# Queries and keys of the two-mixer layers: transposed by VectorE blocks and on-chip transfers in place of TensorE

## What is computed

```python
proj = h @ w_in                       # 256 x 3088
aq, ak, av, gq, gk, gv, gr, g_low = jnp.split(proj, cuts, axis=-1)
aq = rope_partial(aq.reshape(B, S, 8, 64), pos)     # rotates 16 of the 64 numbers of a head
ak = rope_partial(ak.reshape(B, S, 8, 64), pos)
s  = einsum('bqhd,bqnhd->bhqn', aq, keys) * 64 ** -0.5   # masked, dilated; softmax; times values
a_out = rmsnorm(dilated_attention(aq, ak, av).reshape(B, S, 512), attn_out_norm)
o     = gla_chunked(gq, gk, gv, log_sigmoid(g_low @ w_gate_up + b) / 16)
g_out = rmsnorm(o, gla_out_norm) * silu(gr)
return concatenate([a_out, g_out]) @ w_out
```

## Time and profile before

| what | value |
|---|---|
| time, median of 3 runs | 1162.05 us (1161.86 to 1162.26) |
| the profiled execution, its own time | 1161.88 us |
| span of that execution, first to last instruction | 1160.1 us |
| TensorE busy | 1147.4 us, 99% of the span |
| VectorE busy | 779.3 us, 67% |
| ScalarE busy | 604.6 us, 52% |
| mean granted TensorE clock | 0.999 |

### The profile page before, as it was taken

One profiled execution on the slowest core, in us unless ns is written; L12 is line 12 of the kernel. 1 busy time (PEld: TensorE's weight loads), 2 busy tenths in 40 slices (PEclk: granted clock), 3 DMA queues, 4 the chain that ended last, 5 costly groups with the idle time before them and its releaser, 6 DMA issues.

```text
span 1160.1 us, 18219 instructions
## 1 busy us (share of the span) xinstructions
PE 1147.4 (99%) x6746; PEld 938.9 (81%) x6746; DVE 779.3 (67%) x1149; ACT 604.6 (52%) x896; POOL 46.5 (4%) x82
## 2 busy tenths in 40 slices
PE   8999999999999999999999999999999999999998
PEld 6887888888868888888778888888887778888886
DVE  5798666548897865554778777566466877865641
ACT  5555544425964554443556665445356666654530
POOL 0200000000001000000100100000010011000000
PEclk9999999999999999999999999999999999999999
DMA  9756876745734687664575169777548514877650
GB/s 328 252 169 195 277 217 217 218 147 180 254 93 145 203 271 218 217 208 158 166 238 155 33 195 296 218 214 224 163 147 272 164 56 145 275 222 219 211 171 36
DMA packets 186440, 225.82 MB, mean 195 GB/s; under 512 B 15954, under 2 KB 130298, under 8 KB 186369
## 3 DMA queue, kind: packets, MB, share of 16 engines
q1 hardware_dynamic: 181184, 213.07, 58.2%
q10 hardware_dynamic: 4896, 11.58, 3.1%
q0 software_dynamic: 288, 0.23, 0.1%
HBM read 212.22 MB, written 1.06 MB: 184 GB/s over the span
## 4 chain that ended last, share of the span: by engine, by line
PE 49%; DVE 2%; issue 0%; ACT 0%; POOL 0%; POOLq 0%; DVEq 0%; ACTq 0%
PE ps L601 15%; PE ps L603 14%; PE ps L602 14%; DVE w_lo L1602 1%; PE ps L973 1%; PE ps L769 1%; PE ps L1056 1%; PE ps L1031 1%; PE ps L777 0%; PE ps L1003 0%; PE ps L784 0%; PE ps L1023 0%; PE ps L1020 0%; DVE nbuf L1922 0%; PE ps L1002 0%
## 5 line engine op out<-in xcount | busy, mean ns | idle before, releaser
L1602 DVE TENSOR_TENSOR w_lo<-raw,w_hi 128x1024 fp32r<-128x1024 f32 x377 | 445.4, 1216 | 122.2 <-ACT w_hi L1201 119.1
L1201 ACT ACTIVATE w_hi<-raw 128x1024 fp32r<-128x1024 f32 x377 | 383.3, 1056 | 153.0 <-DMA raw<-w_down 35.2
L601 PE MATMUL ps<-w_hi,a_hi 128*128 128x512 f32 x1039 | 409.1, 394 | 2.2 <-DVE w_lo L1602 1.1
L603 PE MATMUL ps<-w_hi,a_lo 128*128 128x512 f32 x1039 | 404.8, 390 | 0.0
L602 PE MATMUL ps<-w_lo,a_hi 128*128 128x512 f32 x1039 | 404.5, 389 | 0.0
L601 PEld LDWEIGHTS ps<-w_hi,a_hi 128*128 128x128 f32 x1039 | 195.0, 188 | 44.7 <-DVE w_lo L1602 2.1
L603 PEld LDWEIGHTS ps<-w_hi,a_lo 128*128 128x128 f32 x1039 | 195.0, 188 | 41.2
L602 PEld LDWEIGHTS ps<-w_lo,a_hi 128*128 128x128 f32 x1039 | 195.2, 188 | 39.1
L601 PE MATMUL ps<-w_hi,h_hi 128*128 128x512 f32 x480 | 188.3, 392 | 0.5 <-DVE h_lo L2092 0.4
L603 PE MATMUL ps<-w_hi,h_lo 128*128 128x512 f32 x480 | 186.9, 389 | 0.0
L602 PE MATMUL ps<-w_lo,h_hi 128*128 128x512 f32 x480 | 186.9, 389 | 0.0
(11 more groups left out here) (224 smaller groups left out, 675.7 us busy)
## 6 DMA issues: line engine op xcount, KB each, us to landing
raw<-ffn_w_in SPq DMA_DIRECT2D x176, 256.0 KB, 4.1
raw<-w_in SPq DMA_DIRECT2D x96, 256.0 KB, 3.7
raw<-ffn_w_out SPq DMA_DIRECT2D x88, 256.0 KB, 3.1
raw<-w_gate SPq DMA_DIRECT2D x88, 256.0 KB, 3.3
raw<-w_up SPq DMA_DIRECT2D x88, 256.0 KB, 4.0
raw<-w_down SPq DMA_DIRECT2D x88, 256.0 KB, 3.2
moved<-turned SPq DMA_DIRECT2D x176, 64.0 KB, 2.6
raw<-od_w_in SPq DMA_DIRECT2D x40, 256.0 KB, 3.8
```

What stands on the lines that cost most here:

```text
L601: nc.tensor.matmul(ps[:, bank, :], hi, wh, start=first, stop=False)
L603: return nc.tensor.matmul(ps[:, bank, :], lo, wh, start=False, stop=last)
L1201: nc.scalar.activation(w_hi[:, v.slot, :], raw[:, v.slot, :], ACT.Copy).then_inc(w_high, 1)
L1602: V.tensor_tensor(w_lo[:, v.slot, :], raw[:, v.slot, :], w_hi[:, v.slot, :].bitcast(F32), ALU.subtract).then_inc(w_low, 1)
```

## The change

Only the two `hyb` layers change; the attention of layer 1 keeps its path (its semaphores are declared for that layer alone now).

- TensorE: the two `turn_qk` of a layer go, with their waits. `pair_logits` reads queries and keys from a new tile, `qk_moved`, after one wait for eight transfers.
- ScalarE: `q_part` goes; the factor -1/8 is put into the copy of chunk 1 from PSUM (`scale` of L1280), ahead of the rotation, which is linear.
- VectorE: `k_part` goes. New is `qk_squares`, at the end of `hyb_step` for c = 2, ahead of its last `feed`: four `transpose` instructions (32x32 blocks within 128x512) from `p_qk` to `qk_turned`. They write each output row of 32 numbers with a step of 64 bytes from one number to the next, since `qk_turned` keeps query or key, pair and token tile as the innermost indices.
- SP: new is `move_qk`, after the seventh unit of `w_out` (i == 6): a wait for `qk_squares`, then eight transfers from `qk_turned` to `qk_moved`, each 64 rows of 2 KB, so 128 KB each and 1 MB in all per layer.
- In `qk_moved` the tokens of one head and one tile are 16 numbers (64 bytes) apart. Both operands of the logits products are read with that step.

```diff
+        qk_moved, _ = place("qk_moved", [P, P, 2, 4, NT], F32)
+        qk_turned, _ = place("qk_turned", [P, 2, 2, 32, 2, 4, NT], F32, at_turned)
...
+            def move_qk(l):
+
+                sp.wait_ge(qk_done.sem, qk_done.at(l, 0))
+                for a in range(4):
+                    for par in range(2):
+                        sp.dma_start(qk_moved[64 * par:64 * (par + 1), 32 * a:32 * (a + 1), :, :, :].rearrange("p j s b t -> p (j s b t)"),
+                                     qk_turned[32 * a:32 * (a + 1), par, :, :, :, :, :].rearrange("p u j s b t -> p u (j s b t)")
+                                     ).then_inc(qk_in, 16)
...
                     load(Unit(U_B[l] + i), wo[k, :, 0:CH], wo[k, :, CH:D], False)
+                    if LAYERS[l] == "hyb" and i == 6:
+                        move_qk(l)
...
-                    if (c, q) == (4, 0):
-
-                        pe.wait_ge(z_out.sem, z_out.at(l, 0))
-                        pe.wait_ge(roped.sem, roped.at(l, 0))
-                        turn_qk(l, 0)
-                    if (c, q) == (5, 0):
-                        pe.wait_ge(q_out.sem, q_out.at(l, 1))
-                        turn_qk(l, 1)
...
+            def queries(l, i, j, t):
+                r = slice(HD * i, HD * (i + 1))
+                if LAYERS[l] == "hyb":
+                    return qk_moved[r, :, 0, j, t]
+                return qT[r, j, P * t:P * (t + 1)]
+
+            def keys(l, i, j, n):
+                r = slice(HD * i, HD * (i + 1))
+                if LAYERS[l] == "hyb":
+                    return qk_moved[r, :, 1, j, 0:n].rearrange("p n t -> p t n")
+                return kT[r, j, 0:P * n]
...
-                pe.wait_ge(q_out.sem, q_out.at(l, 1))
-                pe.wait_ge(k_out.sem, k_out.at(l, 1))
+                pe.wait_ge(qk_in, 128 * (hyb.index(l) + 1))
...
-                nc.scalar.activation(dst, bank, f).then_inc(a_out, 1)
+                scale = -SCALE if (LAYERS[l], c) == ("hyb", 1) else 1.0
+                nc.scalar.activation(dst, bank, f, scale=scale).then_inc(a_out, 1)
...
-                    if n == 5:
-                        q_part(l)
...
+            def qk_squares(l):
+
+                dve.wait_ge(roped.sem, roped.at(l, 0))
+                for part in range(2):
+                    for t in range(NT):
+                        dst = qk_turned[:, :, :, :, part, :, t].rearrange("p r u j b -> p b (r u) j")
+                        ins = V.transpose(dst, p_qk[:, t, CH * part:CH * (part + 1)])
+                        if (part, t) == (1, 1):
+                            ins.then_inc(qk_done.sem, 1)
...
+                if c == 2:
+                    qk_squares(l)
                 if c == 4:
-                    k_part(l)
                     feed(end)
```

More of the change, by code:

```diff
@@ L207, in blocks_kernel @@
         glu, _ = place("glu", [P, 2, NT, FC], F32)
-        turned, _ = place("turned", [P, LOOP, 4, 2, NT, 32], F32)
+        turned, at_turned = place("turned", [P, LOOP, 4, 2, NT, 32], F32)
         moved, _ = place("moved", [P, LOOP, 4, 2 * NT, 32], F32)
+        qk_moved, _ = place("qk_moved", [P, P, 2, 4, NT], F32)
+        qk_turned, _ = place("qk_turned", [P, 2, 2, 32, 2, 4, NT], F32, at_turned)
         assert top[0] <= nc.SBUF_PARTITION_SIZE_BYTES, top[0]
@@ L399, in blocks_kernel @@
         roped = stage("roped", 1, hyb)
-        qk_turned, q_out, k_out = stage("qk_turned", 4, attn), stage("q_out", 2, attn), stage("k_out", 2, attn)
+        qk_by_pe, q_out, k_out = stage("qk_by_pe", 4, [1]), stage("q_out", 2, [1]), stage("k_out", 2, [1])
+        qk_done, qk_in = stage("qk_done", 1, hyb), sem("qk_in")
         logits, lows, weighed = stage("logits", HEADS, attn), stage("lows", HEADS, attn), stage("weighed", HEADS, attn)
@@ L1011, in turn_qk @@
                 for i in range(2):
-                    turn_blocks(2 + i, p_qk, CH * part + 2 * P * i, qk_turned)
+                    turn_blocks(2 + i, p_qk, CH * part + 2 * P * i, qk_by_pe)
             def pair_logits(l, j):
@@ L1018, in pair_logits @@
                 for i in range(2):
-                    r = slice(HD * i, HD * (i + 1))
-                    nc.tensor.matmul(tb[:, i, 0:P], qT[r, j, 0:P], kT[r, j, 0:P], start=True, stop=True)
+                    nc.tensor.matmul(tb[:, i, 0:P], queries(l, i, j, 0), keys(l, i, j, 1), start=True, stop=True)
                 for i in range(2):
-                    r = slice(HD * i, HD * (i + 1))
-                    nc.tensor.matmul(tb[:, i, P:3 * P], qT[r, j, P:SEQ], kT[r, j, :], start=True,
+                    nc.tensor.matmul(tb[:, i, P:3 * P], queries(l, i, j, 1), keys(l, i, j, 2), start=True,
                                      stop=True).then_inc(logits.sem, 1)
+            def queries(l, i, j, t):
[8 more added lines that the diff above has]
+                return kT[r, j, 0:P * n]
             def head_turn(l, h):
@@ L1432, in q_part @@
                 for i in range(2):
-                    act.wait_ge(qk_turned.sem, qk_turned.at(l, i))
+                    act.wait_ge(qk_by_pe.sem, qk_by_pe.at(l, i))
                     nc.scalar.activation(qT[:, 2 * i:2 * i + 2, :], blocks(2 + i), ACT.Copy, scale=-SCALE).then_inc(q_out.sem, 1)
@@ L1446, in k_part @@
                 for i in range(2):
-                    act.wait_ge(qk_turned.sem, qk_turned.at(l, 2 + i))
+                    act.wait_ge(qk_by_pe.sem, qk_by_pe.at(l, 2 + i))
                     nc.scalar.activation(kT[:, 2 * i:2 * i + 2, :], blocks(2 + i), ACT.Copy).then_inc(k_out.sem, 1)
@@ L2023, in hyb_rest @@
                 feed(U_C[l] + 4)
[L2026 to L2029, removed]
             def head_lows(l, h):
```

## The result

The changed kernel takes **1168.88 us** (median of 6 runs, 1167.92 to 1170.5), the kernel before 1161.95 us beside it. The ratio is 1.006, with a 95% interval of 1.005 to 1.0071: slower by 6.9 us, where 2.5 us less was forecast. The profiled execution of it has a span of 1167.0 us and a time of 1168.81 us.

The account below looks back on a forecast made before the run. TensorE, busy 99% of the span, was taken to bound the kernel. Per layer -1.75 + 0.45 = -1.3, two layers -2.6, forecast 1159.5 us against 1162.05; range 1158.4 to 1167.0, this case alone 1158.5 to 1160.5.

Parts of the forecast that it names:

- `turn_qk` goes, -1.75 us a layer: TensorE at hooks (4, 0) and (5, 0): removed transposes save 0.87 and 0.88 us, 3.5 us in all.
- I take nothing: TensorE's logits: 64-byte operand steps cost zero, hidden by a slow column pace; bounds 0 to +6.8 us in all.
- rival 1: Logits read slower on TensorE: a doubling adds 0.85 us for each of eight pairs, 1166.3 us; alone 0.15.
- A transpose at 0.61: VectorE, between two splits before step 5's factors: each new transpose takes 0.61 us, 2.44 us for four.
- rival 2: VectorE's transposes write slower: 0.53 us more each, level 6 stall 2.55, total 1163.7 us, balance 0.93 a transpose; alone 0.15.
- The chain to level 6: VectorE's transposes delay step 5's factors through ScalarE's exponential; TensorE stalls 0.45 us a layer at level 6.
- 1.0 us ahead: VectorE before `two_mixers`: last `keep` ends at about 633.4, 1.0 us ahead of TensorE; cost zero.
- 0.67 and 0.42: True room, in us, left of VectorE's idle times of 1.54 and 1.72 once TensorE comes 0.87 and 1.3 earlier.
- The transfers, zero: SP's eight moves land by 632.3, needed at 634.4; the delayed `w_out` unit is also hidden; cost zero.
- rival 3: Copy arrives late at the `two_mixers` entry: each us over costs 2 us in all; this or another stall 0.08.
- not on the path: ScalarE loses two copies a layer, gains nothing, and the scale rides on an existing copy; effect zero.
- the case of both: Slower logits reads and slower transpose writes together: 1170.5 us, chance 0.12.

Follow-up runs that it names:

- the 8-byte layout without stalls: Changed kernel with the 8-byte layout plus the VectorE order of the first reordered kernel: 1159.59 us, ratio 0.9978 to the kernel before.
- the dense run: Changed kernel with the logits reading neighbouring numbers of the transferred tile (wrong tokens) instead of 64-byte steps: 1162.61 us, ratio 1.0008 to the kernel before.
- the 8-byte layout: Changed kernel with only the two token tiles interleaved, so logits reads and transposes' writes step 8 bytes instead of 64: 1160.70 us, ratio 0.9988.
- the run with the transfers alone: Kernel before plus eight 128 KB transfers per layer from a constant tile, TensorE still transposing: 1162.45 us, ratio 1.0003.
- the first reordered kernel: Changed kernel, 64-byte steps kept, with transposes behind the factors of step 5 and last `keep` ahead of the last split: 1168.57 us, ratio 1.005.

## Why the prediction was wrong, point by point

- **`turn_qk` goes, -1.75 us a layer.** Right: the account closes with it, and in the 8-byte layout without stalls most of it arrives.
- **"I take nothing" for the logits' 64-byte reads.** This is the step that failed, for +5.8 of the 9.4 us between forecast and result; the transposes' writes make 2.2 and the last `keep` 1.1. The bounds were 0 and +6.8; measured are 0.73 on top of 0.85 for each of eight pairs, so rival 1's doubling was nearly right. The reason given, that a logit column is read at less than half of the engine's pace and so leaves room for a slower read, was already wrong in the earlier trace rows. They show four instructions of each kind, where `pair_logits` has two products of each kind. So each product is run in two instructions of its full width: 4 x 128 + 4 x 256 = 1536 columns in 0.85 us, 0.55 ns each, not 768 at 1.1, against 0.45 ns for `fp32r`. There was little slack to hide in, and the dense run shows that the step was not hidden. A slow stretch of an engine is no room for another delay until something shows that the two overlap.
- **A transpose at 0.61, bounds 0.60 to 0.65.** For writes with 8 bytes right, 0.60, and 0.43 us are then lost at level 6 where 0.45 was forecast. With 64 bytes it is 0.89: the forecast left the step to rival 2, which took 0.53 more a transpose and put the balance at 0.93. It costs 0.28 more, 1.1 us of stall a layer. The row by which rival 2 was priced, the last `keep`, has itself a step of only 8 bytes, which costs a transpose nothing; so what makes that copy slow is something else, and no run tests it.
- **The chain to level 6.** The mechanism was right. 4 x 0.28 added to a wait of 0.45 is 1.57, which is the measured loss.
- **The last `keep` "1.0 us ahead", cost zero.** Wrong: it is 0.57 late, and 0.59 in the 8-byte layout. The failed step is the room of "0.67 and 0.42" found in VectorE's idle times. VectorE did have it, but ScalarE didn't: from the exponential of step 6 on it works without a gap, and hands the whole lateness on to step 7. So 0.86 us of VectorE's new room, and of that which `k_part` left, was spent waiting for ScalarE.
- **The transfers, zero.** Right, by the trace (10 us of room) and by the run with the transfers alone. So rival 3 didn't happen.
- **ScalarE, "not on the path".** Right for the two copies, wrong for the exponentials, see above.
- **The rivals.** The outcome is the case of both, 1170.5, given 0.12; the range ended at 1167.0 and left most of that case out. That the number of this case is only 1.6 us off is in part luck: both of its terms were too large, rival 1's a little (6.8 against 5.8) and rival 2's almost twice (4.2 against 2.2), and the 1.1 us of the last `keep` are in neither. The Trainium skill's rule that was cited against the change ("Advanced Engine Details and Errata", Memory Cachelines) held in both places. It had been given 0.42 in all.
- **Unforeseen:** the spread of the changed kernel. A stretch at half clock is shown in one profile, of the first reordered kernel (1.3 us a layer). For the four runs of the changed kernel at 0.996, 1.9 us slower than the rest, it is inferred from their mean clock, since they have no trace. What starts it in some runs and not in others stays open.

## What to carry to other kernels

Lay out what TensorE or VectorE reads or writes in bulk so that at least two float32 numbers of the walk share 16 bytes; if an index must be interleaved, put the one of size two innermost and nothing else. This was tested for block transposes and float32 products alone: the predicated copy of `keep` takes 1.31 us with a step of 8 bytes where it takes 0.78 with runs of eight. When work goes to an engine that already paces a chain, follow that engine's queue to the next place where it is waited for: here the same lateness showed at level 6, then at the entry, then at the second pair, and only less work removed it. And a stall that disappears from one row is a gain only if the time of the next meeting point moves with it.

## What the runs showed of the hardware

- For float32 numbers a step of 8 bytes is almost as good as dense (0.89 against 0.85 for a pair, 712 ns for a transpose either way), one of 16 bytes already costs all that 64 bytes cost, or a little more (1.67 and 1.58; 1082 and 1010 to 1068 ns).
- Both sides of a TensorE product pay: with 64 bytes, loading weights of 128 columns takes 307 ns by duration instead of 188 dense, an instruction of 256 columns 603 instead of 377. Long runs in the moving operand (32 numbers, then a jump) are free, 0.86.
- TensorE's granted clock can fall to half within a kernel that is busy 99% of its span: three to four us at 0.50 behind a wait of 1.24 us, in both layers of the profile with 64-byte reads. In ten runs with a wait of 1.4 us at the same place and 8-byte reads it didn't.
